# Where the weight parts and the activation pairs start in SBUF, modulo 256 bytes

## The reference

```python
proj = h @ w_in                                    # first layer, 1024 -> all branches
branch = jnp.einsum('bsmw,mwd->bsmd', ys, w_branch)
merged = jnp.sum(gates * branch.astype(F32), axis=2).astype(h.dtype)
...
x = x + (jax.nn.silu(h2 @ w_ffn_gate) * (h2 @ w_ffn_up)) @ w_ffn_down   # layers two and three
```

## The kernel before

| tensor | start in bytes, before | modulo 256, before | after |
|---|---|---|---|
| `whi`, `wlo` | 58592, 70880 | 224 | 0 |
| `wraw`, `X` | 46304, 29920 | 224 | 224 |
| `u`, `Ha`, `HH`, `HL`, `HBh`, `HBl`, `yp`, `mp`, `ckp` | (99552 for `HH`) | 224 | 224 |
| `oph` and `opl`, `act2`, `fact` | 174208, 178304, 180352 | 128 | 224 |
| `KBh`, `KBl` | 209920, 214272 | 0 | 96 |
| `cqph`, `cqpl` | 218592, 222688 | 224 | 96 |

## Time and profile before

### The profile page before, as it was taken

How to read it: one execution, slowest core, us unless ns; L and a number is a source line. 1 busy time by engine, 2 the same in 40 slices (tenths; PEclk the granted TensorE clock), 3 DMA queues, 4 the chain that set the end, 5 groups by cost and what they waited for, 6 DMA issues and landing times.

```text
span 3821.5 us, 51932 instructions
## 1 busy us (share of the span) xinstructions
PE 3699.8 (97%) x22058; PEld 2984.5 (78%) x22058; DVE 2144.3 (56%) x3227; ACT 1493.0 (39%) x2593; POOL 72.2 (2%) x92
## 2 busy tenths in 40 slices
PE   8989999899999999999999999999999999999998
PEld 6678688787876887887777888888777778888886
DVE  6865645757444466567575445434665754454345
ACT  5733334335223344343355323223434563232233
POOL 0022000000000000000000000000000000000000
PEclk9999999899999999999999999999998999999999
DMA  3200123032321223333200233232332003333322
GB/s 140 65 3 4 57 94 101 22 105 72 119 96 45 99 89 92 101 94 106 73 1 23 83 98 109 82 110 88 96 101 68 1 28 99 100 102 88 105 87 78
DMA packets 91532, 298.57 MB, mean 78 GB/s; under 512 B 10147, under 2 KB 12707, under 8 KB 90788
## 3 DMA queue, kind: packets, MB, share of 16 engines
q1 hardware_dynamic: 88848, 286.50, 23.3%
q10 hardware_dynamic: 2452, 8.76, 0.7%
HBM read 292.07 MB, written 2.10 MB: 77 GB/s over the span
## 4 chain that ended last, share of the span: by engine, by line
PE 86%; DVE 9%; ACT 4%; issue 1%; DMA 0%; SPq 0%; DVEq 0%; ACTq 0%
PE ps L638 22%; PE ps L640 22%; PE ps L639 22%; PE ps L1264 2%; PE ps L1274 1%; PE psl L1283 1%; DVE wlo L2161 1%; PE ps L1283 1%; ACT whi L1421 1%; PE ps L793 1%; PE ps L677 1%; PE ps L679 1%; PE ps L678 1%; PE ps L798 1%; PE ps L786 1%
## 5 line engine op out<-in xcount | busy, mean ns | idle before, releaser
L2161 DVE TENSOR_TENSOR wlo<-wraw,whi 128x1024 fp32r<-128x1024 f32 (+5 forms) x603 | 663.7, 1103 | 1230.1 <-ACT whi L1421 1220.8
L1421 ACT ACTIVATE whi<-wraw 128x1024 fp32r<-128x1024 f32 (+5 forms) x603 | 576.2, 958 | 1211.0 <-PE ps L640 1136.2
L638 PE MATMUL ps<-HH,whi 128*128 128x512 f32 x1880 | 749.2, 399 | 9.7 <-DVE wlo L2161 7.2
L640 PE MATMUL ps<-HH,wlo 128*128 128x512 f32 x1880 | 733.3, 390 | 0.0
L639 PE MATMUL ps<-HL,whi 128*128 128x512 f32 x1880 | 733.0, 390 | 0.0
L638 PEld LDWEIGHTS ps<-HH,whi 128*128 128x128 f32 x1880 | 353.8, 188 | 98.7 <-issue 12.8
L639 PEld LDWEIGHTS ps<-HL,whi 128*128 128x128 f32 x1880 | 353.8, 188 | 79.5 <-issue 7.5
L640 PEld LDWEIGHTS ps<-HH,wlo 128*128 128x128 f32 x1880 | 353.4, 188 | 74.8
L638 PE MATMUL ps<-HBh,whi 128*128 128x512 f32 x816 | 321.3, 394 | 1.3 <-DVE HBl L2779 0.9
L640 PE MATMUL ps<-HBh,wlo 128*128 128x512 f32 x816 | 318.0, 390 | 0.0
L639 PE MATMUL ps<-HBl,whi 128*128 128x512 f32 x816 | 317.8, 389 | 0.0
(11 more groups left out here) (648 smaller groups left out, 6095.2 us busy)
## 6 DMA issues: line engine op xcount, KB each, us to landing
wraw<-in_w_ff SPq DMA_DIRECT2D x88, 512.0 KB, 3.4
wraw<-in_w_bg SPq DMA_DIRECT2D x48, 512.0 KB, 3.5
wraw<-in_ffn_up SPq DMA_DIRECT2D x44, 512.0 KB, 3.2
wraw<-in_w_z SPq DMA_DIRECT2D x36, 512.0 KB, 3.2
wraw<-in_w_gate SPq DMA_DIRECT2D x32, 512.0 KB, 3.2
wraw<-in_w_br SPq DMA_DIRECT2D x32, 512.0 KB, 3.3
wraw<-in_w_rw SPq DMA_DIRECT2D x26, 512.0 KB, 3.3
wraw<-in_w_mam SPq DMA_DIRECT2D x24, 512.0 KB, 3.2
```

The lines of the kernel that those rows point to most:

```text
L638: MM(b[0:m, :], hi[:, k, c0:c0 + m], x[0], start=(start and k == 0), stop=False)
L640: ins = MM(b[0:m, :], lo[:, k, c0:c0 + m], x[0], start=False, stop=(stop and k == n - 1))
L1421: ACTV(W.pair_of(n)[0], W.raw_of(n), ACT.Copy).then_inc(*up("act", "whi", n))
L2161: TT(l, W.raw_of(n), h.bitcast(F32), SUB).then_inc(*up("dve", "wlo", n))
```

## The change

Two filler tensors are allocated around the high and low weight parts: `step`, 32 bytes, ahead of `whi`, and `stepback`, 224 bytes, behind `wlo`. Together they are 256 bytes, so all later tensors keep their place modulo 256 and only `whi` and `wlo` differ, by 32. `halfpi`, of which one element is used, gets 32 elements: what is stacked on it moves up by 96 bytes. `smc1` gets 32 elements instead of 24: what is stacked on that moves up by 32 more. No instruction is added, removed or reordered.

```diff
-        W = Weights(T, sb(ctx, "wraw", NRAW * SLOT), sb(ctx, "whi", NSPL * SLOT, dt=F32R),
-                    sb(ctx, "wlo", NSPL * SLOT, dt=F32R), known and known["plan"])
+        wraw, _, whi, wlo, _ = (sb(ctx, n, w, dt=t) for n, w, t in (
+            ("wraw", NRAW * SLOT, F32), ("step", 8, F32), ("whi", NSPL * SLOT, F32R), ("wlo", NSPL * SLOT, F32R),
+            ("stepback", 56, F32)))
+        W = Weights(T, wraw, whi, wlo, known and known["plan"])
...
-            HP = sb(c1, "halfpi", 1)
+            HP = sb(c1, "halfpi", 32)[:, 0:1]
...
-                    smC = [sb(c3, "smc%d" % i, 24) for i in range(2)]
+                    smC = [sb(c3, "smc%d" % i, w)[:, 0:24] for i, w in enumerate((24, 32))]
```

## The result

The changed kernel takes 3875.69 us (four runs, 3875.55 to 3878.23) against 3825.45 us before in the same comparison: a ratio of 1.0134, 95% interval 1.0120 to 1.0149. It is slower by 50 us, where 70 us less was forecast.

A forecast was written before the change was run, and what follows sets the result against it. TensorE's queue of 512-wide fp32r matmuls was taken as the bound: number times start-to-start distance. Gains of 44.7 and 27.3 us less costs of 2.0 and 0.5 made 69.5 us off 3825.87: 3756 us, range 3692 to 3835.

The forecast's parts named there:

- the price of displacement 32: Projection matmuls of 512 columns with operands 32 bytes apart modulo 256: forecast one every 222.1 ns.
- lower reading: Surcharge of 5.5 ns plus 1.3 fixed, if part of the 256-wide distance is weight-load pace: 220.1 ns per 512-wide matmul.
- the compression: 256-wide matmuls at L1160 to L1162, price guide at displacement 32; their own move to 96 was to cost 2.0 us.
- displacement 160: Read from the 408-wide rows, half at 0 and half at 160: about 20 ns surcharge for 160 alone.
- first kind: The 9720 projection matmuls, nearly all from displacement 0: 226.7 to 222.1 ns each, 44.7 us less.
- `cqp`: 72 matmuls on `cqp`, which comes to lie at displacement 160: 0.5 us more.
- token-major matmuls: L677 to L679 and L1362 to L1364, weights as moving operand: taken as 0, 512-wide bounds -2.9 to +1.8 us.
- the middle of the two readings: Distance taken for 512-wide matmuls at displacement 32, between 220.1 and 223.9 ns: close to 222.1 ns.
- rival D: Operand places have no effect and the two distances come from something else: 3826 us, chance 0.04.
- the second half's pairs: 2256 matmuls on `act2`, `op` and `fact`, from displacement 96: 7.5 ns less each at 226.7 ns, 16.9 us.
- rival B: Displacement 32 is as good as 0, so only the second half's pairs gain: 3811 us, chance 0.14.
- Rival A: Displacement 32 finds no steady state: 230.0 or 234.2 ns per matmul, 3851 or 3901 us, chance 0.20.

The follow-up runs named there:

- e2: Against the kernel before, only the step of 32 bytes ahead of the weights, with `halfpi` and `smc1` as before: 3872.6 us, ratio 1.0127.
- e3: The kernel of e2 with a step of 64 bytes instead of 32: 3872.11 us.
- e4: The kernel of e2 with a step of 96 bytes instead of 32: 3873.27 us.
- e6: The changed kernel without `stepback`, so weights and activations all lie at 0 modulo 256: 3809.62 us, ratio to before 0.9965.
- e1: The changed kernel with the step ahead of the weights undone, keeping the moves of `halfpi` and `smc1`: 3808.35 us, ratio to before 0.9955.
- e9: Against e1, the moving operand of the projection matmuls is one column read 512 times: 3697.83 us.
- e10: Against e1, weight loads cut to 64 columns in all but the first and last `k` of a tile: 3833.8 us.
- e13: Against e1, weight loads cut to one column in all but the first and last `k` of a tile: 3845.61 us.
- e16: Against the changed kernel, weight loads cut to one column in all but the first and last `k` of a tile: 3861.14 us.
- e11: Against e1, only `wlo` moved, by 192 bytes, so one matmul of three has its weights displaced: 3852.1 us, ratio 1.0072.

## Why the prediction was wrong

**The step that failed** is the price of displacement 32 for a 512-wide matmul. The prediction carried a surcharge of 10.6 ns (and, in its lower reading, 5.5) from the compression, 256 columns wide, to 512 columns, and took 222.1 ns. It is 20.0 ns, and the distance 233.3. The prediction called this its weakest step; what it lacked was the compression at another displacement, which e2 supplied: 281 ns at 0, 280 to 282 at 32, and distances of 118.8 against 118.0. At 256 columns 32 costs no more than 0, at 512 columns 6.6 ns more, so the surcharge read there said nothing about 32 at 512. The row taken was also a low one: 117.3 ns, where the whole group's distances under 200 ns have a mean of 118.0. The prediction had a nearer guide in hand: its own reading of displacement 160 from the 408-wide rows, about 20 ns, is what e3 measured (233.3, a surcharge of 20.0), and 96 had 20.9.

**The sum**, with the measured distance put in: 9720 x 6.6 - 2256 x 0.9 + 2.5 = 64.6 us more. The runs give 50, the profiled executions 52. What is left comes from taking the settled 226.7 for the whole first kind (its mean was 227.2, 5 us; at 32 there is no settling to be lost behind breaks, another 4 us) and from small groups priced too high: the compression was to cost 2.0 us and cost 0.1, `cqp` came out 0.7 us lower where 0.5 more was forecast. The token-major matmuls were given 0, the 512-wide ones within -2.9 to +1.8 us, and rose by 1.1. Two small slips bear on nothing here: the middle of the two readings is 222.0 ns, and half-way between 3756 and 3664 us lies 3710, not 3692.

**Right:** that the kernel's time is the number of the projection matmuls times their distance; that the displacement modulo 256 sets it, or at 16 and 128 which values it can have, and not the place or the load (e4, e6), so rival D is out; that both kinds come to one value; that nothing else changes and no other engine becomes the bound; that the second half's pairs at displacement 0 are worth 16.9 us (e1: 16 to 17), which is the part of rival B that holds.

**Rival A** is what happened, at a price between its two cases (230.0 and 234.2 ns): 233.3. Its reason was half right. Displacement 0 is indeed a special one among all that were tried, but 32 finds a steady pattern too, of two distances, from the first matmul on. It is the value of that pattern which is high.

**The mechanism** behind the prediction, a surcharge for weight reads that the moving stream meets, holds for half of it. The 13.4 ns at displacement 0 are not such a price: they are there only while the moving operand walks (e9), and they do not shrink with 64 weight columns or one (e10, e13). The 6.6 ns between 0 and 32 do need the weight reads: they are gone between loads of one column (e13 and e16, both 231.5). Shown besides: one pair of three displaced shifts the whole stream (e11), and one pair at one displacement can run steadily at two distances (226.7 and 233.3 at 16, 232.3 and 233.3 at 128). A fixed price per matmul can't do that; a repeating timing pattern, of which the displacement allows one or several and the start of the stream picks one, can. That the start picks it was only argued. What in the memory or its read path the moving walk waits for, why 8 bytes suffice to leave the good pattern, and why 192 is better than its neighbours, stays open.

## What to carry to other kernels

Where fp32r matmuls of 512 columns follow each other without idle time, compare the mean of one across the tensors that they read: differences between groups of the same shape point to places in memory, and adding up the allocations modulo 256 shows which. Put stationary and moving operand at the same remainder, exactly; here that was worth 17 us for 2256 matmuls, and in the long streams the eleven other displacements cost 2 to 8 ns per matmul, but for some streams at 16 that lost nothing. One stream is therefore no full measure of a displacement: read several. A price read at one shape is no price for another until the same variable has been seen to matter at that shape.

## What the runs showed of the hardware

- The distance of back-to-back fp32r matmuls of 512 columns at the 2.4 GHz level depends on the displacement of their operands modulo 256: 226.7 ns at 0, 228.9 at 192, 230.7 to 234.3 elsewhere, with two steady values at 16 (226.7, 233.3) and at 128 (232.3, 233.3).
- The distance depends on the moving operand's own reads: 215.8 ns when it stands still, 226.7 when it walks, and 241.9 when it walks within 64 bytes. The Trainium skill (SBUF — State Buffer, section "Who interferes with whom") says that "PE and ACT never wait on anyone". That sentence is on waits for other engines, which no run here tests; it does not mean that a stream has no cost from its own reads.
- A weight load of one column still lasts 82 or 83 ns against 188 for 128 columns and does not make the stream faster (231.5 ns between two such loads against 226.7). Between such loads displacement 32 costs no more than 0.
- Distances settle in short cycles: one value at displacement 0, two alternating ones (231 to 232 and 235 ns) at 32.
